# Mixture-of-experts block: the down matrix by columns, each quarter scattered and added inside its own job

## What is computed

```python
def grouped_moe(x, w_router, router_bias, w_gate, w_up, w_down):
    ...
    combine = jnp.einsum('btk,btke->bte', gates, jax.nn.one_hot(idx, N_EXPERTS, dtype=jnp.float32))
    y = jnp.zeros_like(x)
    for e in range(N_EXPERTS):
        h = jax.nn.silu(x @ w_gate[e]) * (x @ w_up[e])
        y = y + combine[..., e:e + 1] * (h @ w_down[e])
    return y
# and in the layer:
h_l = h_l + mod_l[5] * grouped_moe(m_l, ...)
```

## Time and profile before

| | |
|---|---|
| time, median of 3 runs | 1456.27 us (1454.73 to 1460.87) |
| span of the profiled execution | 1455.7 us |
| TensorE matmuls busy | 1305.8 us (90%) |
| VectorE busy | 431.7 us (30%) |
| ACT busy | 206.0 us (14%) |
| read from HBM | 556.33 MB, 384 GB/s over the span |
| mean granted clock of TensorE | 0.976 |

### The profile page before, as it was taken

One profiled execution on the slowest core, in us unless ns is written; L12 is line 12 of the kernel. 1 busy time (PEld: TensorE's weight loads), 2 busy tenths in 40 slices (PEclk: granted clock), 3 DMA queues, 4 the chain that ended last, 5 costly groups with the idle time before them and its releaser, 6 DMA issues.

```text
span 1455.7 us, 20523 instructions
## 1 busy us (share of the span) xinstructions
PE 1305.8 (90%) x8712; PEld 627.4 (43%) x8713; DVE 431.7 (30%) x827; ACT 206.0 (14%) x481; POOL 74.7 (5%) x138
## 2 busy tenths in 40 slices
PE   3999999999999998999999999997977887878866
PEld 1656544555454565432632543442432442343223
DVE  3122597777656140201111111021110111111112
ACT  3000101244101042200210110110110110011001
POOL 0012100121132000000000000000000000000000
PEclk9899999999999899999999999999999999999988
DMA  9899868766899789999999999999999999999996
GB/s 393 342 420 407 327 257 332 285 229 246 330 359 349 278 356 427 426 428 414 427 426 421 418 425 429 400 428 427 430 427 429 429 428 429 428 430 428 429 427 260
DMA packets 57018, 559.55 MB, mean 384 GB/s; under 512 B 6640, under 2 KB 6768, under 8 KB 19952
## 3 DMA queue, kind: packets, MB, share of 16 engines
q1 hardware_dynamic: 42048, 502.24, 82.6%
q0 software_dynamic: 14320, 52.01, 9.7%
q10 hardware_dynamic: 576, 4.19, 0.7%
HBM read 556.33 MB, written 2.10 MB: 384 GB/s over the span
## 4 chain that ended last, share of the span: by engine, by line
PE 59%; DMA 33%; DVE 4%; issue 2%; ACT 1%; DVEq 0%; POOL 0%; SPq 0%; ACTq 0%; POOLq 0%
DMA ring<-w_up_dram 13%; DMA ring<-w_gate_dram 12%; PE ps L874 10%; PE ps L879 8%; PE ps L597 8%; PE ps L841 5%; PE ps L898 5%; DMA ring<-w_half_dram 3%; PE ps L700 3%; PE ps L904 3%; PE ps L591 3%; PE ps L602 2%; DMA ring<-w_in_dram 2%; DMA big<-w_up_dram 2%; PE ps L510 1%
## 5 line engine op out<-in xcount | busy, mean ns | idle before, releaser
L1585 DVE TENSOR_TENSOR big<-ps,big 128x1024 f32<-128x1024 f32 x60 | 70.7, 1220 | 309.0 <-PE ps L827 163.0
L879 PE MATMUL ps<-ring,big 128*64 128x512 f32 x560 | 131.2, 601 | 21.8 <-DMA ring<-w_up_dram 10.6
L597 PE MATMUL ps<-ring,big 128*128 128x512 f32 x320 | 145.3, 596 | 2.0 <-DMA ring<-w_in_dram 2.0
L1230 DVE SCALAR_TENSOR_TENSOR once<-ring,silu_c,once 128x1024 f32<-128x1024 f32 x96 | 123.2, 1283 | 66.3 <-DMA ring<-w_half_dram 61.2
L841 PEld LDWEIGHTS ps<-probs,big 128*128 128x128 f32 x1024 | 120.2, 193 | 44.2 <-issue 37.5
L841 PE MATMUL ps<-probs,big 128*128 128x96 f32 x1024 | 130.6, 281 | 1.9 <-DVE probs L1589 1.9
L874 PE MATMUL ps<-ring,early 128*32 128x256 f32 x1408 | 92.3, 412 | 34.0 <-DMA ring<-w_up_dram 17.6
L700 PE MATMUL ps<-ring,big 128*128 128x512 f32 x256 | 116.0, 611 | 0.0
L597 PEld LDWEIGHTS ps<-ring,big 128*128 128x128 f32 x320 | 58.7, 190 | 71.2 <-issue 66.4
L879 PEld LDWEIGHTS ps<-ring,big 128*64 128x64 f32 x560 | 35.8, 136 | 103.0 <-issue 65.6
L874 PEld LDWEIGHTS ps<-ring,early 128*32 128x32 f32 x1408 | 45.0, 116 | 81.0 <-issue 27.3
(11 more groups left out here) (308 smaller groups left out, 1133.9 us busy)
## 6 DMA issues: line engine op xcount, KB each, us to landing
ring<-w_down_dram SPq DMA_DIRECT2D x48, 2048.0 KB, 22.9
ring<-w_up_dram SPq DMA_DIRECT2D x46, 2048.0 KB, 22.8
ring<-w_gate_dram SPq DMA_DIRECT2D x33, 2048.0 KB, 21.7
ring<-w_half_dram POOLq DMA_DIRECT2D x96, 512.0 KB, 6.6
big<-w_up_dram SPq DMA_DIRECT2D x18, 2048.0 KB, 21.5
ring<-w_mix_dram SPq DMA_DIRECT2D x32, 1024.0 KB, 11.6
late<-w_down_dram SPq DMA_DIRECT2D x16, 2048.0 KB, 23.1
big<-w_gate_dram SPq DMA_DIRECT2D x15, 2048.0 KB, 24.5
```

Source lines behind the costliest of these rows:

```text
L597: mm = pe.matmul(ps[:, b + t, :], nT[:, k, t * P:(t + 1) * P], w, start=(k == 0), stop=(k == KT - 1))
L879: mm = pe.matmul(out_b[1][REST * f:REST * (f + 1), :], rows[1][:, k, :], w[:, kk, f * N:(f + 1) * N], start=(k == 0), stop=(k == KT - 1))
L1230: stt(total, half_slots[:, m % HALF_SLOTS, :], silu_c[:, m % KT, 0:1], total, ALU.mult, ALU.add) \
L1585: tt(y, Yb[:, 2 * h:2 * h + 2, :].rearrange("p a n -> p (a n)"), y, ALU.add).then_inc(summed, 1)
```

## The change

w_down is stored by columns. Each pair of chunks now holds all 1024 rows of 512 columns, a *quarter* of the output; a chunk is four blocks of 128 rows. So after each pair one quarter is complete. The four column groups of the array (two for part 1) now take different blocks of rows of the same quarter; their partial sums lie in different partitions. The scatter contracts over all 128 partitions and so adds them up too. It runs inside the job: quarter q after the first chunk of quarter q+1, the last one at the job's end. VectorE multiplies a quarter by the gate row and adds two pieces of 512 columns to total, and SP sends the quarters of the last job as they are added. Gather has two banks (`Xb`) and scatter two (`Yb`); a gather waits until ACT has emptied its bank (`rows_saved`). The gate row is broadcast to all 128 partitions.

```diff
-        Gb, Ub, Db = [ps[:, 1, 0:256], ps[:, 0, :]], [ps[:, 3, 0:256], ps[:, 2, :]], [ps[:, 0, :], ps[:, 2:4, :]]
+        Gb, Ub = [ps[:, 1, 0:256], ps[:, 0, :]], [ps[:, 3, 0:256], ps[:, 2, :]]
+        Db = [[ps[:, 2, :], ps[:, 1, :]], [ps[:, 0, :], ps[:, 3, :]]]
-        Yb = ps[:, 4:8, :]
+        Xb, Yb = ps[:, 4:6, :], ps[:, 6:8, :]
...
-            for q, (t, a, b) in enumerate(OUT_PIECES):
-                sp.wait_ge(out_ready, q + 1)
-                sp.dma_start(out[t * P:(t + 1) * P, a:b], total[:, t, a:b]).then_inc(out_sent, 16)
+            for q in range(4):
+                for t in range(TT):
+                    sp.wait_ge(summed, jobs * 8 + (2 * q + t + 1))
+                    sp.dma_start(out[t * P:(t + 1) * P, q * N:(q + 1) * N], total[:, t, q * N:(q + 1) * N]) \
+                        .then_inc(out_sent, 16)
...
+                    for n in range(2):
+                        q = 2 * i + n
+                        mm = pe.matmul((S if i else C)[n], k_("spread")[:, q * P:(q + 1) * P], modrow[:, 1, :],
+                                       start=True, stop=True)
...
+            def scatter(j, q, parts, first):
+
+                pe.wait_ge(outs_saved, j * 4 + (q + 1))
+                if q == 0:
+                    pe.wait_ge(spread_saved, j + 1)
+                if q or not first:
+                    pe.wait_ge(summed, j * 8 + (2 * q + 8))
+                for t in range(TT):
+                    for i in parts:
+                        mm = pe.matmul(Yb[:, t, :], spread_T[i][:, t, :], outs[i][q % 2],
+                                       start=(i == parts[0]), stop=(i == parts[-1]))
+                    mm.then_inc(scattered, 1)
...
+                for q in range(4):
+                    if q >= 2:
+                        pe.wait_ge(outs_saved, j * 4 + (q - 1))
+                    elif q == 1 and 1 in parts:
                         pe.wait_ge(spread_saved, j + 1)
+                    for c in range(2):
+                        w = arrived(16 + 2 * q + c).rearrange("p (k n) -> p k n", k=4)
+                        for i in range(4) if 0 in parts else ():
+                            k = 4 * c + i
+                            at = (k % 2) * P + BASE * (k // 2)
+                            mm = pe.matmul(Db[0][q % 2][BASE * i:BASE * (i + 1), :], hT[0][:, at:at + BASE], w[:, i, :],
+                                           start=(c == 0), stop=(c == 1))
+                        for i in range(4) if 1 in parts else ():
+                            k = 4 * c + i
+                            at = (k % 4) * P + REST * (k // 4)
+                            mm = pe.matmul(Db[1][q % 2][REST * (i % 2):REST * (i % 2 + 1), :], hT[1][:, at:at + REST],
+                                           w[:, i, :], start=(k < 2), stop=(k >= 6))
+                        mm.then_inc(slot_free, 1)
+                        if c == 0 and q:
+                            scatter(j, q - 1, parts, first)
+                    if place != "second":
+                        for i in ((0, 1), (2,), (3,), ())[q]:
+                            gather(j + (2 if place == "lead" else 1), i, oh_rows, first)
+                scatter(j, 3, parts, first)
...
+                for q in range(4):
+                    cols = slice(q * N, (q + 1) * N)
+                    dve.wait_ge(slot_free, j * JCH + used_job(17 + 2 * q))
+                    for i in parts:
+                        last = tt(outs[i][q % 2], Db[i][q % 2], gate_b[:, cols], ALU.mult)
+                    last.then_inc(outs_saved, 1)
+                    for t in range(TT):
+                        dve.wait_ge(scattered, j * 8 + (2 * q + t + 1))
+                        tt(total[:, t, cols], Yb[:, t, :], total[:, t, cols], ALU.add).then_inc(summed, 1)
...
-        "w_down": a["w_down"].reshape(NE, 4, 2, P, D).transpose(0, 1, 3, 2, 4).reshape(NE, 4, P, 2 * D),
+        "w_down": a["w_down"].reshape(NE, 8, P, 4, N).transpose(0, 3, 2, 1, 4).reshape(NE, 4, P, 2 * D),
```

More of the change, by code:

```diff
@@ L809, in table, with gather @@
                 mm.then_inc(table_done, 1)
[L811 to L833, removed]
+            def scatter(j, q, parts, first):
[9 more added lines that the diff above has]
+                    mm.then_inc(scattered, 1)
+            def gather(j, i, one_hot, first=False):
                 if i == 0:
                     pe.wait_ge(oh_ready, j)
-                pe.wait_ge(summed, adds)
+                if i > 1 or not first:
+                    pe.wait_ge(rows_saved, j * 4 + (i + 3))
                 for k in range(4 * i, 4 * i + 4):
@@ L840, in gather, with experts @@
                     for t in range(TT):
-                        mm = pe.matmul(Yb[:, i, at:at + BLK], tokens[:, t, k * P:(k + 1) * P], one_hot[:, t, :],
+                        mm = pe.matmul(Xb[:, i % 2, at:at + BLK], tokens[:, t, k * P:(k + 1) * P], one_hot[:, t, :],
                                        start=(t == 0), stop=(t == TT - 1))
                 mm.then_inc(next_gathered, 1)
-            def experts(j, parts, first=False, place=None, ahead=(0, 1)):
+            def experts(j, parts, first=False, place=None):
                 def arrived(i):
@@ L882, in experts @@
                         if place == "lead" and m == 0 and i in (1, 3, 4, 5):
-                            gather(j + 1, (1, 3, 4, 5).index(i), oh_second, j * 4)
-                if not first:
-                    scatter(j, 1, parts=ahead)
+                            gather(j + 1, (1, 3, 4, 5).index(i), oh_second)
                 pe.wait_ge(hidden_ready, j + 1)
@@ L937, in _ @@
                     experts(i * 2 + 1, (0,), place="lead")
-                    experts(i * 2 + 2, (0, 1), place="second", ahead=(0,))
+                    experts(i * 2 + 2, (0, 1), place="second")
             pairs, mid_pairs = count(2), count(3)
@@ L942, in _ @@
                     experts(i * 2 + 1, (0,), place="lead")
-                    experts(i * 2 + 2, (1,), place="second", ahead=(0,))
+                    experts(i * 2 + 2, (1,), place="second")
             rest = count(4)
@@ L1129, in save_rows_of @@
             def save_rows_of(j, to):
[L1130 to L1136, removed]
+                for i in range(4):
+                    act.wait_ge(next_gathered, j * 4 + (i - 3))
+                    for k in range(4 * i, 4 * i + 4):
+                        at = k % 4 * BLK
+                        last = act.activation(to[:, k, :], Xb[:, i % 2, at:at + BLK], ACT.Identity,
+                                              bias=modcol[:, 3, k, 0:1], scale=scale_ffn[:, k:k + 1])
+                    last.then_inc(rows_saved, 1)
             def job_evac(j, parts, first=False, place=None):
@@ L1595, in hidden_product @@
                     one_hot_rows(j + 1, oh_second)
-                spread_matrix(j, 0, "slots_w" if 1 in parts else "slots_n")
-                spread_matrix(j, 1, "slots_m" if 1 in parts else "slots_0")
-                if not first:
-                    add_rows(j, 0)
+                if 0 in parts:
+                    spread_matrix(j, 0, "slots_w" if 1 in parts else "slots_n")
+                if 1 in parts:
+                    spread_matrix(j, 1, "slots_m")
                 dve.wait_ge(silu_saved, j + 1)
@@ L1658, in _ @@
                     any_job(j, False)
-            for t, a, b in OUT_PIECES:
-                dve.wait_ge(scattered, jobs * 4 + (2 * t + a // 1024 + 1))
-                banks = ps[:, 0:4, :] if t else Yb
-                tt(total[:, t, a:b], banks[:, a // N:b // N, :].rearrange("p a n -> p (a n)"), total[:, t, a:b],
-                   ALU.add).then_inc(out_ready, 1)
 def kernel(**inputs):
```

92 lines of the change are left out of this document (18 added, 74 removed).

## The result

The changed kernel takes 1518.3 us (median of 4 runs, 1513.3 to 1522.7), the kernel before beside it 1458.1 us (1454.7 to 1460.9): a ratio of 1.0417, 95% interval 1.0387 to 1.0446, 60 us more. The forecast was 1510 us, in a range of 1496 to 1524. The profiled execution has a span of 1518.8 us, 63.1 more than that of before.

A forecast was written before the change was run, and what follows sets the result against it. TensorE was taken to bind the expert stage's first half, transfers the second. +8 (job 0), +48.9 (three pairs), −2 (buffers) and −1 (end) gave +54 on 1456 us: 1510 us, range 1496 to 1524.

The forecast's parts named there:

- What bounds: Expert stage: TensorE sets the time in jobs 1 to 6, transfers bind in jobs 7 to 14.
- Rival A: Expert stage: transfers set the end and added matmuls fill idle time; 1455 us, not slower; chance 0.04.
- The price of a full-height matmul: Scatter over all 128 rows and 512 columns: 0.86 us per matmul, about 0.15 per change of shape.
- The pairs: Jobs 1 to 6, a lead and a second job each: +16.3 us a pair, +48.9 for three.
- The second job: Second job of a first-half pair, running the scatter of both parts after the change: +14.8 us.
- The lead of the later pairs: First job of a first-half pair, running part 0's scatter after the change: +1.5 us.
- the −0.6 for the wait for the one-hot matrix: Lead job's first gather: its 0.6 us wait for VectorE goes, as additions and the wide product leave there.
- Job 0: First expert job: its own scatter 7.8 us and a 0.9 wait; +7.0 to +8.7, taken as +8.
- What the buffers give back: Before job 7: half a load won once as transfers run ahead, −2 us (0 to −5).
- The end: After the last up pair: loop exit and most additions saved, scatters paid; −1 us (0 to −3).
- Rival B: First-half pairs: leads catch up, only the excess over the loads is paid, 4 us each; 1473 us; chance 0.06.
- Rival C: Six job ends in the first half: the new wait stops the sequencer running ahead, about 15 more, 1525 us; chance 0.10.

The follow-up runs named there:

- the size experiment: Kernel before, with each scatter matmul contracting over all 128 rows instead of its own 32 or 64, at the old place: 1500.6 us, ratio 1.0319.
- the fillers: Changed kernel with 12 or 24 idle full matmuls added to each of four lead jobs in the second half: 1520.9 us (1.0450) or 1548.1 us (1.0606).
- the kernel with 128 columns: Changed kernel with its scatter matmuls streaming 128 of the 512 columns of a quarter, waits and places kept: 1475.7 us, ratio 1.0132.

## Why the prediction was right, and where it was not

The sign and the mechanism held: the first half is bound by TensorE, and the scatter lost its packing. Its two large terms were met, each by a measurement of its own.

- *What bounds.* Right, and it is the step that decided. Rival A (the transfers cover the scatter) falls by the size experiment alone, 46 us at the old place. The picture of two halves holds: about 12 us a pair to spare in the second (the fillers), none in the first (13.2 us expected for the larger scatter, 12.9 measured).
- *The price of a full-height matmul.* 3.63 us for four and a change of shape, 3.6 in the sum. Right.
- *The pairs.* +50.0 against +48.9. The second job +15.0 against +14.8. The lead of the later pairs +2.2 against +1.5 (137.4 less 88.3 makes 49.1, 46.9 before). The term that failed is the −0.6 for the wait for the one-hot matrix. VectorE does have it earlier (its last row for it, L1563, ends at 718.14), but TensorE stands all the same, 1.02 and 0.63 us, and it does so one record into the gather, behind the one wait for that matrix. The profile shows nothing that it waits for.
- *Job 0.* +8.4 and +1.2, together +9.6 against +8. The step that failed is the size of the standing time. The last scatter does run beneath it, as the sum assumed: with 0.71 us of scatter instead of 1.98 (the kernel with 128 columns) TensorE stands 7.4 us instead of 5.8. But from the wait for the last product to job 1 it takes 7.8 us (571.10 to 578.90), and the sum had the 4.6 us of the earlier trace rows for all of it. Why it is 7.8 was not tried.
- *What the buffers give back.* This step failed, −2 forecast and +2.9 measured. The size experiment shows that the argument itself held: there the stretch from job 6's last product to the landing is 488.9 us (962.72 to 1451.57) against 491.0 before, 2.2 less, as forecast. What it left out is the state in which the second half begins: the buffers are full, and while TensorE stands in job 7 or runs at the lower clock few of them come free (39 GB/s from 995 to 1000 us). Filling that gap brought 2.6 of the 4.9 us back, in one execution; what the other 2.3 are stays open.
- *The end.* −2.5 against −1, within its bounds of 0 to −3. From the landing of the last up load the last addition ends after 29.9 us (1485.7 to 1515.6), and the sum had 29.9 (1420.15 to 1450.0): loop exit, scatters and additions were counted right. What it left out is the output: from the last addition to the end it takes 3.2 us instead of 5.1, and a piece of the output lands 2.5 us after its issue instead of 3.8 (medians).
- *Rival B* falls by the pairs: each cost 16.7 us on average, not 4. The leads do catch up with the transfers, but the next second job uses that up.
- *Rival C* (0.10) had a real cause and a price that was too high. Behind each second job of the first half TensorE stands while the profile shows nothing that it waits for: 1.0, 0.6 and, where the loops change, 3.2 us; behind a lead it does not. The kernel with 128 columns shows that the last scatter covers most of it, as the argument against C said: with 2.5 us less of scatter it stood 2.3 to 2.7 us more. So it cost 4.9 us and the low clock behind the last gap, not 15. That the sequencer is what is late is inferred from the missing releaser; no run tried it.

Of the 9 us between the 54 of the sum and the 63 of the profile, 3.1 are the start of job 0, 1.6 job 0 and the gap behind it, 1.1 the pairs, and 4.9 the buffers with job 7's gap, less 1.5 at the end. The sum came within 6 us of the 60 measured, with no error of a large term hidden by another; but the start of job 0 alone moves by more than that from one execution to the next.

## What to carry to other kernels

Before a step is moved to where its result is ready, look at what made it cheap where it was: here four row groups of the array shared one streaming time because their sums were already complete, and a layout that leaves partial sums in different partitions pays for them with full-height matmuls (3.63 us instead of 1.07 for part 0, 3.43 instead of 1.92 for part 1). Split a stage by jobs before saying what bounds it: a share of transfers of 1.00 stood over a half in which no matmul waited for a transfer. Where two bounds lie within 2%, adding to the one that sets the end costs in full while taking from it gives next to nothing. And when an experiment takes work away, look for waits that this work had covered before adding up the parts.

## What the runs showed of the hardware

- Scatter matmuls of 32 rows in four row groups took 1.07 us for four, the same at full height 3.63. With 128 columns streamed instead of 512 a full-height float32 matmul took 0.27 us, less than its two weight loads would give at the 0.19 us each of the earlier trace rows; eight of them took 0.97 us here.
- A gap of 3.2 us in which TensorE waits for nothing that the profile shows left the granted clock at 0.50 for about 10 us (2.4 to 1.2 GHz); with four matmuls queued ahead of it the gap was 0.6 us and the clock stayed at 1.00. Five such matmuls behind job 0 stood behind a gap of 4.5 us and took 6.3 us instead of 4.3, in part at the lower clock.
- The mixing half, the same in all kernels, ended anywhere in 11 us (524.9 to 535.7) over ten profiled executions, while two pairs of one execution agreed to 0.4 us (137.6 and 137.2).
- From the wait for a second job's last product to TensorE's next gather it took 6.2 to 7.0 us, whether 1.15 or 3.69 us of scatter were queued behind the wait; what the scatter did not cover was stood.
